# A mixed mLSTM, attention and expert layer: bias by VectorE, opening loads and router rearranged, and the first expert's products between the gathers

## The chip, the cores and the metric

The kernel runs on one core of one Trainium2 chip. The metric is the device time of one execution in microseconds (us); lower is better. Engines are named TensorE (PE in the profile), VectorE (DVE), ScalarE (ACT), GpSimd (POOL) and SyncE (SP, which here only issues transfers).

## The reference

One decoder layer over 256 tokens of 2048 channels, all in fp32:

```python
h = rms_norm(x, norm1_g); z = h @ w_in              # 2048 x 11272
qk = silu(causal_dwconv([qm, km], conv_w))          # 4 taps
hm = sigmoid(om) * head_layernorm(mlstm(q, k, v, i, f))     # 4 heads of 256
ha = softmax(q @ k.T * dh**-0.5 + bias[rel_bucket]) @ v     # 8 heads of 128, causal
y = sigmoid(gm) * (hm @ w_branch_m) + sigmoid(ga) * (ha @ w_branch_a)
x = x + y @ w_out
t = rms_norm(x, norm2_g)
# group top-1 of 4, expert top-2 of 8 in it; 32 SwiGLU experts 2048 -> 256 -> 2048
x = x + sum_e w_e * (silu(t @ w1[e]) * (t @ w3[e])) @ w2[e]
out = rms_norm(x, final_g)
```

## The kernel before

All instructions are written out by hand for each engine; semaphores order them, and nothing is scheduled by a planner. An engine runs its instructions in the order of its own function.

**Projections.** The weights of `w_in`, the two branch matrices and `w_out` come in units of 256 columns, and each unit in two halves of 1024 rows (1 MB). SP loads a half into one of four raw buffers `wraw` (L395), ScalarE rounds it to fp32r in one of two buffers `wsplit` (L581), VectorE stores the remainder beside it (L1149, `split_half`), and TensorE multiplies the activations' two parts with the weights' two parts: two instructions for each of 8 row chunks, of 512 and 256 columns (`channel_half` L824, L826; `token_half` L840, L842). The two column halves of a bank are added by VectorE afterwards (L1158, `sum_halves`). TensorE takes some 5.5 us for a half.

**Opening.** ScalarE's queue issues nine small loads (L559 to L567: norm and convolution parameters, the gates' weight columns `wif_raw`, a broadcast bias `ifb`, the relative bias table, the bucket matrix and `g2T`). SP loads x in two halves and waits for all nine before the first weights (L389). ScalarE squares x (L572), GpSimd takes the root (L519), TensorE turns x with a diagonal matrix (L813), and `act_split` holds the normed, turned x. TensorE also spreads the bias table over distances with the bucket matrix (L803); VectorE copies the row (L1178), and SP stores it to DRAM and reads it back as `bias_flipped`, one shifted copy for each partition (L409, L412).

**Attention loop** (L908 on, four turns, each with two attention heads, one mLSTM head and eight halves of the gates' weights, `gate_half`). For each attention head TensorE adds the bias to the logits by products with a flip matrix (L920, L922); VectorE takes the maximum (L1324, L1325) and ScalarE the exponential (L662, L664).

**Output projection and router.** Eight units of `w_out`. For each, VectorE adds x (L1449, `x2u`), ScalarE copies it to `x2` and squares it (L725, L729), TensorE turns it (L984), ScalarE copies that (L713), and TensorE multiplies with the router's weights (L993) into a place for each unit. Then VectorE adds the units (L1496), scales with the root of the mean square (L1502), and chooses group and experts in some thirty short steps (`first_of` L1486 to L1490). ScalarE makes `h2n` and `h2hi` (L744, L746), GpSimd and VectorE the remainder `h2lo` (L552, L1528). TensorE ranks the tokens (L1026 to L1030), and VectorE makes the selection matrix `sel` (L1539 to L1542).

**Gather and experts.** 16 gathers (L1043), each four products of 512 columns into one of eight banks, bring the tokens into the order of their experts; ScalarE and VectorE copy the banks to `xg` in turn (L757, L1567). Where no expert has over 64 tokens, the short branch runs (`by_most` L360): 16 pairs of experts, in each `hidden` (L1056, w1 and w3, with two half-array products for each of 16 chunks), the gate, `rows` (L1084, w2) and `scatter` (L1100, L1101) of the pair before. SP loads w1 and w3 of an expert in an upper and a lower half of the rows (2 MB each), as TensorE gets done with the halves before, and w2 into two slots.

## Time and profile before

| | |
|---|---|
| median of 3 runs | 1272.96 us (1272.76 to 1274.13) |
| the profiled execution | 1268.82 us |
| its span | 1267.3 us |
| mean granted TensorE clock | 0.986 |
| busy: PE / PEld / DVE / ACT / POOL | 1183.3 / 886.9 / 689.1 / 413.2 / 44.9 us |
| moved by DMA | 336.52 MB, mean 266 GB/s |

The profile is one execution of the program. A row of the timeline gives start and length of an instruction and, in brackets, how long its engine had been idle and what ended that. Waiting of an engine costs time only where the others wait for it in turn. All times in the rows are from the span's start; the projections last to about 750 us, the router to 775, the gather to 791, and the experts to the end.

### The profile page before, as it was taken

Reading aid. Unit: us, or ns where it says so; the run is one execution under the profiler, and the core shown is the slowest. Engines: PE = TensorE matmul, PEld = TensorE weight load, DVE = VectorE, ACT = ScalarE, POOL = GpSimd, SP = SyncE. Lnnn points to the kernel's source line nnn. Section 1 sums busy time; section 2 is a strip of 40 time slices with the busy share of each in tenths; the row PEclk is TensorE's granted clock in tenths of the full one; section 3 lists DMA queues with packets and bytes.
Section 4 is the critical chain, followed back from the end, with each engine's and each line's share of the span. In section 5 each row is a group of like instructions: output and inputs, shape, how many; then the busy total and the mean of one; then the engine's idle time right before and its main releaser. Section 6 shows DMA issues by size and latency. Waiting matters only on the chain.

```text
span 1267.3 us, 19180 instructions
## 1 busy us (share of the span) xinstructions
PE 1183.3 (93%) x7194; PEld 886.9 (70%) x7194; DVE 689.1 (54%) x980; ACT 413.2 (33%) x463; POOL 44.9 (4%) x57
## 2 busy tenths in 40 slices
PE   5999999999999999999999985899999999899995
PEld 4888888888888888888888875555554544444442
DVE  4678555554666657567875547243444433433335
ACT  4444333334334354443344443111111211111113
POOL 1000000001002022000000002000000000000000
PEclk9999999999999999999999987999999999999998
DMA  7765565655555455555765635899999999999993
GB/s 245 226 190 175 166 193 172 195 174 178 185 165 167 134 164 165 165 166 182 251 177 181 236 148 226 342 402 425 426 426 425 425 425 425 425 425 424 425 425 150
DMA packets 170146, 336.52 MB, mean 266 GB/s; under 512 B 12144, under 2 KB 136192, under 8 KB 153088
## 3 DMA queue, kind: packets, MB, share of 16 engines
q1 hardware_dynamic: 163088, 335.58, 71.8%
q10 hardware_dynamic: 7024, 0.48, 0.4%
q8 instruction: 22, 0.36, 0.1%
q14 instruction: 12, 0.10, 0.0%
HBM read 333.93 MB, written 2.11 MB: 265 GB/s over the span
## 4 chain that ended last, share of the span: by engine, by line
PE 56%; issue 39%; ACT 1%; DVE 1%; ACTq 1%; POOL 1%; POOLq 0%; DVEq 0%
PE ps L824 19%; PE ps L840 11%; PE ps L826 10%; PE ps L842 6%; PE ps L973 5%; PE ps L974 2%; PE ps L813 1%; POOL h2lo L552 1%; PE ps L942 0%; PE ps L993 0%; ACTq L564 0%; DVE wsplit L1149 0%; ACT xsq L572 0%; ACT h2n L744 0%; ACT wsplit L581 0%
## 5 line engine op out<-in xcount | busy, mean ns | idle before, releaser
L1149 DVE TENSOR_TENSOR wsplit<-wraw,wsplit 128x2048 fp32r<-128x2048 f32 x120 | 277.1, 2309 | 180.5 <-ACT wsplit L581 179.7
L824 PE MATMUL ps<-act_split,wsplit 128*128 128x512 f32 x1024 | 360.7, 397 | 0.0
L581 ACT ACTIVATE wsplit<-wraw 128x2048 fp32r<-128x2048 f32 x120 | 230.0, 1917 | 386.7 <-PE ps L826 204.7
L826 PE MATMUL ps<-act_split,wsplit 128*128 128x256 f32 x1024 | 286.6, 280 | 0.0
L840 PE MATMUL ps<-wsplit,act_split 128*128 128x512 f32 x640 | 226.8, 398 | 2.1 <-DVE wsplit L1149 2.1
L824 PEld LDWEIGHTS ps<-act_split,wsplit 128*128 128x128 f32 x1024 | 192.0, 188 | 46.1 <-DVE wsplit L1149 1.3
L826 PEld LDWEIGHTS ps<-act_split,wsplit 128*128 128x128 f32 x1024 | 193.3, 189 | 0.2
L842 PE MATMUL ps<-wsplit,act_split 128*128 128x256 f32 x640 | 179.2, 280 | 0.0
L840 PEld LDWEIGHTS ps<-wsplit,act_split 128*128 128x128 f32 x640 | 120.1, 188 | 31.3 <-issue 2.7
L1056 PE MATMUL ps<-w_a,xe 128*64 128x256 f32 x1024 | 115.4, 381 | 13.8 <-DMA w_a<-in_w_dram 12.0
L1595 DVE TENSOR_TENSOR hid<-sg,ps 128x128 f32<-128x128 f32 x32 | 9.2, 288 | 206.0 <-ACT sg L769 206.0
L842 PEld LDWEIGHTS ps<-wsplit,act_split 128*128 128x128 f32 x640 | 120.8, 189 | 0.0
L1056 PE MATMUL ps<-w_b,xe 128*64 128x256 f32 x1024 | 115.8, 381 | 0.0
L1056 PEld LDWEIGHTS ps<-w_a,xe 128*64 128x64 f32 x1024 | 72.5, 137 | 61.6 <-DMA w_a<-in_w_dram 21.2
L1084 PE MATMUL ps<-w_a,hidT 128*64 128x512 f32 x256 | 113.3, 595 | 0.4 <-ACT hidT L772 0.4
L1084 PE MATMUL ps<-w_b,hidT 128*64 128x512 f32 x256 | 113.3, 595 | 0.0
L1056 PEld LDWEIGHTS ps<-w_b,xe 128*64 128x64 f32 x1024 | 71.3, 137 | 41.6 <-issue 4.3
L1620 DVE TENSOR_TENSOR x<-x,ps 128x512 f32<-128x512 f32 x128 | 85.0, 684 | 9.0 <-PE ps L1101 6.8
L973 PE MATMUL ps<-br_split,wsplit 128*128 128x512 f32 x256 | 88.8, 394 | 0.0
L1084 PEld LDWEIGHTS ps<-w_a,hidT 128*64 128x64 f32 x256 | 33.7, 137 | 70.0 <-issue 68.9
L1100 PE MATMUL ps<-ys_hi,slot_of 128*128 128x512 f32 x128 | 61.0, 477 | 18.8 <-DVE x L1620 18.8
L769 ACT ACTIVATE sg<-ps 128x128 f32<-128x128 f32 x32 | 8.9, 277 | 198.4 <-PE ps L1056 198.4
(274 smaller groups left out, 1082.0 us busy)
## 6 DMA issues: line engine op xcount, KB each, us to landing
w_a<-in_w_dram SPq DMA_DIRECT2D x96, 1024.0 KB, 19.0
w_b<-in_w_dram SPq DMA_DIRECT2D x96, 1024.0 KB, 21.3
wraw<-in_w_in_dram SPq DMA_DIRECT2D x88, 1024.0 KB, 5.1
wraw<-in_w_out_dram SPq DMA_DIRECT2D x16, 1024.0 KB, 5.1
wraw<-in_w_branch_m_dram SPq DMA_DIRECT2D x8, 1024.0 KB, 5.1
wraw<-in_w_branch_a_dram SPq DMA_DIRECT2D x8, 1024.0 KB, 5.1
xin<-in_x_dram SPq DMA_DIRECT2D x2, 1024.0 KB, 6.5
x<-in_x_dram SPq DMA_DIRECT2D x1, 2048.0 KB, 9.3
```

What stands on the lines that cost most here:

```text
L581: act.activation(wsplit[:, q % 2, :, 0], wraw[:, q % RAW], ACT.Copy).then_inc(rounded, 1)
L824: pe.matmul(banks[b], w[:, k, 0, b * P:(b + 1) * P], a, start=first and k == 0, stop=False)
L826: last = pe.matmul(banks[b][:, 0:T], w[:, k, 1, b * P:(b + 1) * P], a[:, 0], start=False, stop=last_half and k == HALF_K - 1)
L840: pe.matmul(banks[t], a[:, 0, t * P:(t + 1) * P], w[:, k], start=first and k == 0, stop=False)
L842: last = pe.matmul(banks[t][:, 0:UNIT], a[:, 1, t * P:(t + 1) * P], w[:, k, 0], start=False, stop=last_half and k == HALF_K - 1)
L973: pe.matmul(bank, w[:, k, 0, b * P:(b + 1) * P], a, start=k == 0, stop=False)
L974: last = pe.matmul(bank[:, 0:T], w[:, k, 1, b * P:(b + 1) * P], a[:, 0], start=False, stop=k == HALF_K - 1)
L1056: last = pe.matmul(ps[f * SLOTS:(f + 1) * SLOTS, 0, 0:2 * P].rearrange("p (w f) -> p w f", w=2), xe[:, b, k], w13[b][:, :, k, f * P:(f + 1 ...
L1084: last = pe.matmul(ps[b * SLOTS:(b + 1) * SLOTS, 2 + n], hidT[:, b, f * SLOTS:(f + 1) * SLOTS], w2s[slot][b][:, f, n * 512:(n + 1) * 512], ...
L1100: pe.matmul(ps[:, 6 + g % 2], to_tokens, ys_hi[:, n * 512:(n + 1) * 512], start=True, stop=False)
L1149: dve.tensor_tensor(wsplit[:, q % 2, :, 1], wraw[:, q % RAW], wsplit[:, q % 2, :, 0].bitcast(F32), ALU.subtract).then_inc(split, 1)
L1620: dve.tensor_tensor(cols, cols, ps[:, 6 + g % 2], ALU.add).then_inc(added, 1)
```

## The change

1. *Opening.* ScalarE issues four loads, the other five follow the first four weight loads on SP (`late_loaded`). VectorE squares the second half of x. The product with the bucket matrix stands behind the first four halves, the copies for it and for the gates behind the first pair of convolution units. Twelve products of the identity with itself (`WARM`) stand ahead of all. The bias row goes to DRAM and back behind the twelve following weight loads.
2. *Attention.* The flip matrix goes. VectorE adds `bias_at` to the logits, reading and writing backwards along the row; ScalarE's exponential reads the sum from SBUF.
3. *Output projection and router.* ScalarE and VectorE split the unnormed x2 into `x2hi` and `x2lo`, unit by unit. The router's products add up over the units in two banks. The last unit's halves of a bank are no longer summed: it takes three products of 256 columns in place, and VectorE adds x to the bank and squares the sum. GpSimd's subtraction (`h2lo`) goes. The starts of the experts come from a scan over the counts.
4. *Gather.* As x2 isn't normed, a product with the roots (`rms_rep`) gives a factor for each slot, `slot_rms`; the tokens are multiplied with it when taken from `xg`. There are 17 gathers over six banks. The first expert's chunk products run three gathers behind.
5. *Loads.* w1 and w3 lie by halves, so the second expert's upper half can be loaded once two raw buffers are free. w2 of experts 1, 2 and 3 is loaded ahead of the gather, that of expert 0 behind it.

The core of the diff:

```diff
 @block.sync
-            sp.wait_ge(par_loaded, 16 * 9)
             pair(COL_QK, None)
+            sp.dma_start(wif_raw[:], ...).then_inc(late_loaded, 16)
...
+            pairs(1, UNITS_QK, COL_QK, 0)
             sp.wait_ge(rev_ready, 1)
             sp.dma_start(rev_dram, rev[:]).then_inc(rev_stored, 16)
             sp.wait_ge(rev_stored, 16)
-            pairs(1, UNITS_QK, COL_QK, 0)
...
             for kh in range(2):
                 load_hidden(0, 0, kh)
-            sp.wait_ge(used, HALVES)
-            for kh in range(2):
-                load_hidden(1, 1, kh)
-            load_rows(0, lambda b: b)
+            for kh in range(2):
+                sp.wait_ge(split, HALVES + 2 * kh - 2)
+                load_hidden(1, 1, kh)
+            sp.wait_ge(used, HALVES - 1)
+            load_rows(0, lambda b: b, (1,))
+            sp.wait_ge(used, HALVES)
+            load_rows(1, lambda b: b + 2, (1,))
             sp.wait_ge(routed, 1)
+            sp.wait_ge(x2lo_ready, UNITS_OUT)
             load_rows(1, lambda b: b + 2, (0,))
-            sp.wait_ge(xg_summed, DC)
-            load_rows(1, lambda b: b + 2, (1,))
 @block.tensor
+            for n in range(WARM):
+                pe.matmul(ps[:, 6, 0:P], ident[:], ident[:], start=True, stop=True)
-                    pe.matmul(bank[:, 0:P], q_h[:, 0:P], k_h[:, 0:P], start=True, stop=False)
-                    pe.matmul(bank[:, 0:P], flip[:], bias[:, 0, P:T], start=False, stop=True)
-                    pe.matmul(bank[:, P:REV], q_h[:, P:T], k_h[:], start=True, stop=False)
-                    pe.matmul(bank[:, P:REV], flip[:], bias[:, 0], start=False, stop=True).then_inc(logits, 1)
+                    pe.matmul(bank[:, 0:P], q_h[:, 0:P], k_h[:, 0:P], start=True, stop=True)
+                    pe.matmul(bank[:, P:REV], q_h[:, P:T], k_h[:], start=True, stop=True).then_inc(logits, 1)
+            def gather_with_first_hidden():
+                done = 0
+                for n in range(COMMON_GATHERS, DC + 1):
+                    gather(n)
+                    if gathers[n] is not None and gathers[n] >= BEHIND:
+                        first_hidden(done)
+                        done += 1
+                for k in range(done, DC):
+                    first_hidden(k)
 @block.gpsimd
-                pool.tensor_tensor(h2lo[:, t, cols], h2n[:, t, cols], h2hi[:, t, cols].bitcast(F32),
-                                   ALU.subtract).then_inc(h2lo_ready, 1)
 @block.vector
+                    dve.tensor_tensor(prob[:, a, P - 1::-1], ps[:, 4 + a, P - 1::-1], bias[:, 0:P], ALU.add)
+                    steps.done(dve.tensor_tensor(prob[:, a, REV - 1:P - 1:-1], ps[:, 4 + a, REV - 1:P - 1:-1], bias[:, 0:T],
+                                                 ALU.add))
...
-            dve.tensor_tensor(mk[:, :, 0], oh[:, :, 0], oh[:, :, 1], ALU.add)
-            steps.done(dve.tensor_tensor(rt[:, 1], iota_t, by_token(FIRST, EXPERTS), ALU.is_gt))
-            dve.tensor_tensor(mk[:, :, 1], rt[:, 3], rt[:, 1], ALU.add).then_inc(mk_ready, 1)
+            dve.tensor_tensor(mk[:], oh[:, :, 0], oh[:, :, 1], ALU.add).then_inc(mk_ready, 1)
...
-                    dve.tensor_copy(xe[:, b], xg[:, :, ds(at, SLOTS)]).then_inc(xe_ready, 1)
+                    factors = slot_rms[:, ds(at, SLOTS)].unsqueeze(1).to_broadcast([P, DC, SLOTS])
+                    dve.tensor_tensor(xe[:, b], xg[:, :, ds(at, SLOTS)], factors,
+                                      ALU.mult).then_inc(xe_ready, 3 - len(experts))
```

How the order of instructions changes at three places. First SP's queue at the start, before (L388 is x, L395 the weight halves):

```order
L388 DMA xin<-in_x_dram 128x2048 x2
L395 DMA wraw<-in_w_in_dram 128x8x256 [waits par_loaded]
L395 DMA wraw<-in_w_in_dram 128x8x256 x3
L409 DMA rev_dram<-rev 8x384 [waits rev_ready]
L412 DMA bias_flipped<-rev_dram 128x256 [waits rev_stored]
L412 DMA bias_flipped<-rev_dram 128x256 x7
```

and now:

```order
L401 DMA xin<-in_x_dram 128x2048 x2
L407 DMA wraw<-in_w_in_dram 128x8x256 x4
L419 DMA wif_raw<-in_w_in_dram 128x16x8
L420 DMA ifb<-in_if_bias_dram 128x8
L421 DMA relb<-in_rel_bias_dram 32x8
L422 DMA onehot_s<-in_onehot_dram 32x256
L423 DMA g2T<-in_norm_g_dram 128x16
```

The first weights wait for nothing, and store and reloading of the bias row are gone from here. On TensorE at the start, before:

```order
L802 MATMUL ps<-ident,param_rows 128x104 [waits par_loaded,consts_ready]
L803 MATMUL ps<-onehot_s,relb 8x256
L813 MATMUL ps<-diag,xin 128x128 [waits normed,x_loaded_1,x_loaded_0,rev_ready,param_ready]
L813 MATMUL ps<-diag,xin 128x128 x31
L824 MATMUL ps<-act_split,wsplit 128x512 [waits split,bank_free]
```

and now:

```order
L834 MATMUL ps<-ident 128x128 [waits ident_ready]
L834 MATMUL ps<-ident 128x128 x11
L836 MATMUL ps<-ident,param_rows 128x104 [waits par_loaded]
L845 MATMUL ps<-diag,xin 128x128 [waits x_loaded_1,normed,x_loaded_0,param_ready]
L845 MATMUL ps<-diag,xin 128x128 x31
L856 MATMUL ps<-act_split,wsplit 128x512 [waits split,bank_free]
```

The turning of x no longer stands behind the bias row (`rev_ready`). On TensorE at the end of the gather, before (`w_a` holds w1 and w3 of the first expert):

```order
L1043 MATMUL ps<-sel,h2lo 128x512
L363 TENSOR_LOAD most_i [waits table_ready]
L363 ISA x2
L364 COMPARE_AND_BRANCH
L1056 MATMUL ps<-w_a,xe 64x256 [waits w13a_upper_loaded,hid_ready,xe_ready]
L1056 MATMUL ps<-w_a,xe 64x256 x15
```

and now, one of the thirteen stretches (`xe_first` holds the first expert's tokens, chunk by chunk):

```order
L1098 MATMUL ps<-sel,x2hi 128x512 [waits gathered_even]
L1098 MATMUL ps<-sel,x2lo 128x512
L1098 MATMUL ps<-sel,x2hi 128x512
L1098 MATMUL ps<-sel,x2lo 128x512
L1113 MATMUL ps<-w_a,xe_first 64x256 [waits first_xe_ready]
L1113 MATMUL ps<-w_a,xe_first 64x256
```

The branch with its load of `most_i` now stands behind the third gather, and the first expert's 32 products come in pairs between the gathers.

## Rows read from the trace of the kernel before

**Rows 1.** By stage: stretch, length, busy PE PEld DVE ACT POOL, PEclk, DMA share, GB/s.

```profile
400.00:560.00 160.00, 160.00 (x923) 139.90 (x922) 101.62 (x163) 70.37 (x76) 16.37 (x15) 1.00 0.50 157
900.00:1200.00 300.00, 278.28 (x1893) 148.52 (x1891) 120.93 (x226) 51.38 (x85) 0.00 (x0) 1.00 1.02 425
```

**Rows 2.** Timeline of the opening: start, length, engine, line, operation, [idle before].

```profile
3.50 4.80 ACTq L564 DMA_DIRECT2D ifb<-in_if_bias_dram  x1
11.06 1.91 ACT L572 ACTIVATE xsq<-xin 128x2048 f32<-128x2048 f32 x1
14.98 0.17 DVE L1163 TENSOR_SCALAR stat<-stat 128x2 f32<-128x2 f32 x1 [8.70 <-ACT xsq L572]
17.06 8.85 PE L813 MATMUL ps<-diag,xin 128*128 128x128 f32 x64 [4.57 <-DVE rev L1178]
```

**Rows 3.** Timeline of TensorE in one turn of the attention loop.

```profile
407.29 0.39 PE L920 MATMUL ps<-bias_flipped,flip 128*128 x2
407.51 0.60 PE L921 MATMUL ps<-qk_now 128*128 128x256 f32 x2
407.95 0.59 PE L922 MATMUL ps<-bias_flipped,flip 128*128 x2
```

**Rows 4.** Timeline of VectorE from the last output unit to the mask.

```profile
750.83 1.29 DVE L1158 TENSOR_REDUCE osum<-ps 128x256 f32<-128x512 f32 x2 [6.32 <-PE ps L842]
752.16 0.69 DVE L1449 TENSOR_TENSOR x2u<-x,osum 128x512 f32<-128x512 f32 x1
756.85 0.82 DVE L1496 TENSOR_REDUCE rt<-ps 128x72 f32<-128x288 f32 x2 [1.86 <-issue]
762.08 4.10 DVE L1521 TENSOR_TENSOR sc<-sc 128x2 f32<-128x2 f32 x1
766.10 2.57 DVE L1486 SCALAR_TENSOR_TENSOR rt<-rt,sc,iota_e 128x32 f32<-128x32 f32 x2
769.61 0.22 DVE L1525 TENSOR_TENSOR mk<-rt 128x64 fp32r<-128x64 f32 x1
```

**Rows 5.** Timeline of GpSimd at the router.

```profile
761.66 6.80 POOL L552 TENSOR_TENSOR h2lo<-h2n,h2hi 128x2048 fp32r<-128x2048 f32 x2 [5.90 <-ACT h2hi L746]
```

**Rows 6.** The instructions that read x's tile, and its load's time to landing.

```profile
L813 PE MATMUL ps<-diag,xin x64: 274/275/552, 17.1 to 25.6; 128*128 128x128 f32 x64
DMA to landing us min/median/max: 5.0/6.5/7.9
```

**Rows 7.** Costliest groups of the page: VectorE's split of a weight half.

```profile
L1149 DVE TENSOR_TENSOR wsplit<-wraw,wsplit 128x2048 fp32r<-128x2048 f32 x120 | 277.1, 2309 | 180.5 <-ACT wsplit L581 179.7
```

**Rows 8.** Timeline of VectorE in the same turn of the loop.

```profile
412.91 0.41 DVE L1325 TENSOR_REDUCE stat<-ps 128x1 f32<-128x256 f32 x1
417.79 1.29 DVE L1158 TENSOR_REDUCE gates<-ps 128x512 f32 x2 [3.94 <-PE ps L826]
```

**Rows 9.** Waits of SP's queue, 0 to 60 us. Columns: total, times, longest.

```profile
SPq L412 <- DMA rev_dram<-rev: 5.5, 1, 5.5
```

**Rows 10.** Timeline of TensorE from the gather to the second expert.

```profile
774.96 0.80 PE L1043 MATMUL ps<-sel,h2hi 128*128 128x512 f32 x1 [3.79 <-DVE sel L1542]
778.25 0.40 PE L1043 MATMUL ps<-sel,h2hi 128*128 128x512 f32 x1
791.30 0.39 PE L1043 MATMUL ps<-sel,h2lo 128*128 128x512 f32 x1
793.43 7.13 PE L1056 MATMUL ps<-w_a,xe 128*64 128x256 f32 x64 [1.74 <-DVE xe L1581]
801.99 7.13 PE L1056 MATMUL ps<-w_b,xe 128*64 128x256 f32 x64
```

**Rows 11.** Timeline of TensorE, first whole-array product behind an expert's half-array products.

```profile
824.75 0.50 PE L1100 MATMUL ps<-ys_hi,slot_of 128*128 128x512 f32 x1
```

**Rows 12.** Costliest groups of the page: weight loads of one expert.

```profile
L1056 PEld LDWEIGHTS ps<-w_a,xe 128*64 128x64 f32 x1024 | 72.5, 137 | 61.6 <-DMA w_a<-in_w_dram 21.2
```

**Rows 13.** One stretch: length, busy PE (x), PEclk, DMA share, GB/s.

```profile
820.00:822.00 2.00, 2.00 (x22) 1.00 0.05 20
```

More of the change, by code:

```diff
@@ L51 @@
 PAIR_HALVES = 4
+WARM = 12
 UNITS_QK = 2 * M_WIDTH // UNIT
@@ L497, in _ @@
                 pool.sem_inc(primed, 1)
-            for m in (ident, flip, before, mask_ts, mask_st, pick):
+            steps.done(pool.memset(ident[:], 0.0))
+            pool.affine_select(out=ident[:], in_=ident[:], compare_op=ALU.not_equal, fill=1.0, base=0,
+                               pattern=[[-1, P]], channel_multiplier=1).then_inc(ident_ready, 1)
+            for m in (before, mask_ts, mask_st, pick):
                 last = pool.memset(m[:], 0.0)
@@ L1015, in _ @@
             pe.wait_ge(wrt_ready, 1)
-            with pe.Fori(1, UNITS_OUT // 2) as i:
+            out_pair(1)
+            with pe.Fori(2, UNITS_OUT // 2 - 1) as i:
                 out_pair(i)
+            out_pair(UNITS_OUT // 2 - 1, end=True)
+            route(UNITS_OUT // 2 - 1, 0)
             turn_x2(1, UNITS_OUT - 1)
-            for u in range(2):
-                last = route(UNITS_OUT // 2 - 1, u)
-            last.then_inc(routed, 1)
+            route(UNITS_OUT // 2 - 1, 1).then_inc(routed, 1)
@@ L1037, in _ @@
-            parts = [part[:].rearrange("p t (q c) -> p t c q", c=DC) for part in (h2hi, h2lo)]
-            for c in range(DC):
-                if c >= 8:
-                    pe.wait_ge((xg_act, xg_dve)[c % 2], (c - 8) // 2 + 1)
-                for t in range(TT):
-                    for n, part in enumerate(parts):
-                        last = pe.matmul(ps[:, c % 8], part[:, t, c], sel[:, t], start=t == 0 and n == 0,
-                                         stop=t == TT - 1 and n == 1)
-                last.then_inc(xg_summed, 1)
+            pe.wait_ge(x2lo_ready, UNITS_OUT)
@@ L1105, in experts @@
                 if chunks > 1:
+                    for n in range(COMMON_GATHERS, DC + 1):
+                        gather(n)
                     with pe.Fori(0, EXPERTS // 4) as j:
@@ L1116, in experts @@
                     return
-                for b in range(2):
-                    hidden(0, 0, b)
-                    turn(0, b)
+                gather_with_first_hidden()
+                turn(0, 0)
+                hidden(0, 0, 1)
+                turn(0, 1)
                 rows(0, 0, 0)
@@ L1302, in _ @@
             dve.wait_ge(o_ready, 1)
-            with steps.loop(0, M_HEADS, 9) as i:
+            dve.wait_ge(flip_loaded, 16 * A_HEADS)
+            with steps.loop(0, M_HEADS, 11) as i:
                 def ahead(q):
```

314 lines of the change are left out of this document (205 added, 109 removed).

## The prediction

> **What bounds the kernel now.** I read the busy time by stage first. While the projections run, TensorE has no gap: 160.00 us of 160 at 400 to 560 us, VectorE at 101.62 and the DMA engines at half their time. From 900 to 1200 us the DMA engines stand at 1.02 of their time and move 425 GB/s, with TensorE at 278 of 300 [rows 1]. So the kernel has two bounds, TensorE up to the router and the stream of expert weights behind it, and between them, at 750 to 820 us, neither: a chain over VectorE, ScalarE, GpSimd and short products. What the change takes from TensorE before the router counts in full. What it takes from the chain counts as far as it lets the weight stream start earlier, since from there the bytes set the end.
>
> Three places matter. **The opening:** ScalarE's queue is held 4.80 us by the issue of the bias load at 3.50, so its first square starts only at 11.06. The mean squares are complete at 14.98, and TensorE turns x from 17.06 [rows 2]. **The attention loop:** each of 8 heads has two products with the flip matrix [rows 3]. **The router:** VectorE's step at 762.08 takes 4.10 us for 128x2 elements and the next pair 2.57 at 766.10, while GpSimd subtracts from 761.66 to 768.46 [rows 4, 5].
>
> **The change, part by part** (gains are minus).
>
> *Opening, -4.5.* x's second half was issued at 1.3 and its load took at most 7.9 [rows 6], so it landed by 9.2. ScalarE now issues four loads, and squares the first half alone. VectorE squares the second in about 2.3 us (its 128x2048 split, [rows 7]): 11.5. From the mean square to the first transpose was 2.08 us, in which the copies of the parameters and of the bias row stood too; those are gone from there, so 1.5. TensorE starts at 13.0, or 12.3 if x lands 0.7 earlier without the small packets beside it. Between the two I take 12.6, so -4.5. Bounds: -3.5 (full 2.08, no earlier landing) and -6.2, where x lands early and the transposes begin at full rate. They now begin at half: one lasts up to 552 ns against 275 in the middle [rows 6]. The 12 warming products run from about 3 us and then TensorE idles for some 5 us, as it did before; I take nothing for them. The first weight load moves from 11 us to 1.7 us and is ready before TensorE asks. Behind the four weight loads stand the late loads. Their first reader on TensorE comes after four halves, at some 43 us, so they cost nothing; if they were late, TensorE would wait there.
>
> *The bucket product, +0.4,* now stands in TensorE's full stretch: 256 columns take 0.44 us as L921 to L922 show [rows 3].
>
> *Bias on VectorE, -5.2.* The product of 128 columns holds TensorE 0.22 us (407.29 to 407.51), the one of 256 columns 0.43 to 0.44. That is 0.65 for a head, 8 heads, 5.2 us. VectorE gains four additions per loop turn; as the maximum over the same 256 columns takes 0.41 [rows 8] and over 128 columns about 0.3, they take 1.4 us. Behind them VectorE sat idle 3.94 us until TensorE was done [rows 8], so they are covered; without that cover they would cost 1.4 a turn. Bounds: -3.9 (a third of a microsecond lost each turn) and -5.3. What was loaded through DRAM at the start moves behind twelve weight loads. SP waited 5.5 us for that store [rows 9]; with the issue of store and bias loads I put it at 8 us on the next weight load. Its slot falls free some three halves of 5.5 us before TensorE needs it, so it is hidden, with about 8 us to spare.
>
> *Small edits before the router, +0.3:* two casts of 128x128 now stand ahead of a split that TensorE waits for. The extra splits of x2 (0.69 each, [rows 4]) and the second copies on ScalarE fall into idle time of 2 to 4 us per half; if it were gone, each would cost its own length.
>
> *Router to choice, -8.5.* The last unit is summed in place: 1.29 and 0.69 [rows 4] become about 0.85, of which the product for the unit before, still in TensorE's order, leaves 0.9. The 0.82 for unit sums at 756.85 and one of two pairs of scalings go, 1.25. Together -2.2. Without GpSimd's subtraction, the pair of rows at 762.08 and 766.10 shrinks from 6.6 us to 0.6, and two comparisons ahead of the mask go: from 762.08 to the mask's end (769.83) 7.75 becomes 1.35, with 0.15 before it, so -6.5. The scan of starts adds 0.2.
>
> *Gather, +5.0.* Before, it was 27.0 us from the first gather product at 774.96 to the second expert's first at 801.99 [rows 10]. Now: 64 products at 0.237 (778.25 to 791.30, 55 steps), 15.1; 1.5 lost in a slow start (eight steps took 3.3); two fp32 row products of 512 columns, 1.7, and the short one 0.4; the first expert's products, 7.1 as at 793.43; the branch, which now stands between gathers, 0.5 (between 0 and the 1.7 it could hide in before); and 13 switches between whole-array and half-array products. One such switch at 824.75 lengthens the first product from 0.40 to 0.50 [rows 11]; with the way in I take 0.25 each, 3.2. That is 29.5. Then the gap before the second expert: 1.4 before, and about 1.1 more, because VectorE now makes the second expert's tokens (128x1024 with a factor, some 1.2) and the mixing after the gather, ahead of the gate. So 32.0 against 27.0.
>
> The switches' bounds are 0 and what full exposure of the weight loads costs: 16 pairs of products, 4 loads of 137 ns each [rows 12], 8.8 us. In a long run the trace shows them hidden: 64 loads of 137 ns in 7.13 us [rows 10]. The Trainium skill (TensorE: Matmul & The Clock Gate, The mechanism) says that a weight load overlaps a running product only when its row group differs, and here all have all rows. The long run doesn't agree with it, but a lone pair is not a long run.
>
> *From there to the end, 0.* The stream waits once more for TensorE: at 820 to 822 the DMA share is 0.05 [rows 13]. As both kernels have loaded the same by then, that restart, and with it the end, moves with the second expert's start. Router plus gather: -8.5 + 5.0 = -3.5 (bounds -8.2 and +2.1).
>
> **Sum:** -4.5 + 0.4 - 5.2 + 0.3 - 3.5 = **-12.5 us**. Against the profiled execution's own 1268.82 that is 1256.3. That execution lies 4.1 below the median of the runs shown, 1272.96, and I put the forecast against the median: **1260.5**.
>
> **Rivals.** (1) *The interleaving eats its gain:* each pair's weight loads are exposed, 8.8 for my 3.2, +5.6: 1266.1. For it, the skill's rule; against it, the long run. 0.15. (2) *All goes through:* switches and branch cost next to nothing, the gap stays at 1.4, and the transposes start at full rate: -3.2, -0.5, -1.1, -1.7 more, 1254.0. For it, products in the trace that switch width without a visible idle time. 0.15. (3) *The 6 us at the router are not GpSimd's:* something else holds VectorE there, and the steps stay long. Then 6.0 less is gained, 1266.5. Against it, the two rows begin and end with GpSimd's two. 0.05. (4) *Slower than before:* the additions write and read backwards. If a step backwards is much dearer than forwards, VectorE comes late in each of four loop turns, and TensorE stands. VectorE has 3.9 us idle and 1.4 us of additions planned; beyond 5.3 us for the four, each further microsecond costs four. It turns the result when they take about 5.3 + 12.5 / 4 = 8.4 us, six times my estimate, and at 9.5 us gives 1277. No row has a backward step, so only implausibility speaks against it: 0.03. That the interleaving doesn't happen at all is excluded by the order of instructions above.
>
> **How the numbers follow.** The forecast has 0.62. The range takes in rivals 1 and 3 nearly whole and most of rival 2: 1254.5 to 1266.5. A measurement of this kernel tells 0.2% (2.5 us) from no change. My own case and rivals 1 to 3 all gain over 6 us; several small misses at once could leave under 2.5, 0.02. So faster 0.95, same 0.02, slower 0.03.
>
> **What would show it.** TensorE's first transpose at 12 to 13.5 us instead of 17.06. The loop of four turns 1.3 us shorter per turn, with VectorE's idle time before the first gate sums near 2.5. No VectorE step over 1 us between the router and the mask, and the first gather product 8.5 us nearer to the last product of the output projection. The second expert's first product 32 us after the first gather product; 37 speaks for rival 1, 28 for rival 2. One gap in the stream of some 3 us, then 425 GB/s. I am wrong if TensorE shows idle time before a reader of the late loads, or at the loads behind the bias, or if the stream restarts no earlier against the router than before.

## The result and the profile after

| | before | changed |
|---|---|---|
| median of 5 runs, us | 1272.96 (1268.77 to 1274.13) | 1262.77 (1260.68 to 1264.67) |
| ratio to before | | 0.9924, 95% [0.9905, 0.9942] |
| the profiled execution, us | 1268.82, span 1267.3 | 1262.77, span 1261.0 |
| mean granted clock | 0.986 | 0.986 |

By the ratio the change is faster by 9.7 us (7.4 to 12.1). The forecast was 12.5 us of gain and 1260.5; the measured median lies 2.3 us above it and inside the range. The two traces differ by only 6.3 us, because the profiled execution of before was as fast as the fastest of its five. Stage by stage they say more than the total does:

| stage, by TensorE's and VectorE's rows | before | after | difference | predicted |
|---|---|---|---|---|
| start to first weight product | 25.67 | 22.66 | -3.0 | -4.5 |
| to the first logits of the attention loop | 328.02 | 330.98 | +3.0 | +0.4 |
| to the last unit's sums | 397.14 | 392.21 | -4.9 | -4.9 |
| to the selection (first product on it) | 24.13 | 14.66 | -9.5 | -8.5 |
| to the second expert's first product | 27.03 | 34.24 | +7.2 | +5.0 |
| to the end | 465.3 | 466.2 | +0.9 | 0 |

Stages of the changed kernel (stretch, length, busy PE PEld DVE ACT POOL, PEclk, DMA share, GB/s); they answer to [rows 1]:

```profile
8.00:13.00 5.00, 0.41 (x2) 0.14 (x1) 2.88 (x6) 1.80 (x1) 0.71 (x1) 0.80 1.09 386
13.00:18.00 5.00, 4.62 (x22) 4.65 (x23) 3.41 (x5) 1.78 (x5) 0.00 (x0) 0.51 1.09 386
...
400.00:560.00 160.00, 160.00 (x921) 139.70 (x920) 108.08 (x177) 73.23 (x77) 16.39 (x15) 1.00 0.52 164
755.00:760.00 5.00, 1.25 (x5) 1.14 (x5) 4.46 (x17) 0.00 (x0) 0.00 (x0) 0.50 0.53 136
...
765.00:770.00 5.00, 5.00 (x23) 3.61 (x22) 2.31 (x6) 1.38 (x2) 0.00 (x0) 0.96 0.01 3
...
900.00:1200.00 300.00, 277.79 (x1874) 147.56 (x1874) 129.73 (x226) 48.98 (x83) 0.00 (x0) 1.00 1.02 425
```

The two bounds are as before: TensorE without a gap up to the router, the weight stream at 425 GB/s behind it. New is the granted clock of 0.51 at 13 to 18 us; 0.50 is the lower of TensorE's two levels (1.2 GHz), 1.00 the upper (2.4 GHz).

The timeline of TensorE in the changed kernel, for [rows 2, 10]:

```profile
2.92 5.18 PE L834 MATMUL ps<-ident 128*128 128x128 f32 x24 [2.92 <-POOL ident L539]
8.91 0.31 PE L836 MATMUL ps<-ident,param_rows 104*128 104x104 f32 x1 [0.81 <-DMA param_rows<-in_norm_g_dram]
13.38 9.52 PE L845 MATMUL ps<-diag,xin 128*128 128x128 f32 x64 [4.17 <-DVE diag L1268]
22.66 0.48 PE L856 MATMUL ps<-act_split,wsplit 128*128 128x512 f32 x1
...
766.80 0.40 PE L1098 MATMUL ps<-sel,x2lo 128*128 128x512 f32 x1
767.13 0.65 PE L1113 MATMUL ps<-w_a,xe_first 128*64 128x256 f32 x4
767.71 0.61 PE L1098 MATMUL ps<-sel,x2hi 128*128 128x512 f32 x1
768.16 0.40 PE L1098 MATMUL ps<-sel,x2lo 128*128 128x512 f32 x1
...
790.69 1.95 PE L1113 MATMUL ps<-w_a,xe_first 128*64 128x256 f32 x16
794.52 0.30 PE L1160 MATMUL ps<-ident,hid 128*128 128x128 f32 x1 [1.89 <-DVE hid L1722]
```

Read the starts. Inside a kind the gather's products follow each other by 0.24 us. Into the first expert's four it is 0.33 (766.80 to 767.13), from there to the next gather product 0.58 against 0.45 for four in a long run (7.13 us for 64), and from that to its successor 0.45. So a step, four gather products and the first expert's four, takes 1.83 us and not 1.39: 0.44 for each pair of switches, out of the gather and back into it.

The last eight products of the router, in the changed kernel and then in the kernel before:

```profile
749.13 1.08 PE L1037 MATMUL ps<-wrt,x2T 128*128 128x36 f32 x8 [0.75 <-ACT x2T L742]
```

```profile
754.84 1.92 PE L993 MATMUL ps<-wrt,x2T 128*128 128x36 f32 x8 [0.24 <-ACT x2T L713]
```

The same eight last 1.08 us in six of the fourteen traces of this study and 1.55 to 1.93 in eight, and one program does both: the kernel before has 1.92, experiment 1 with the same router 1.08. So 0.8 us of the stage from the sums to the selection is chance.

VectorE's timeline in the changed kernel, for [rows 4, 8]:

```profile
9.44 2.28 DVE L1263 SCALAR_TENSOR_TENSOR xsq<-xin 128x2048 f32<-128x2048 f32 x1
...
12.76 0.48 DVE L1268 TENSOR_SCALAR diag<-ident,stat 128x128 f32<-128x128 f32 x2 [0.83 <-POOL stat L560]
...
411.02 0.41 DVE L1421 TENSOR_TENSOR prob<-ps,bias_at 128x256 f32<-128x256 f32 x1
...
415.10 1.29 DVE L1248 TENSOR_REDUCE gates<-ps 128x512 f32 x2 [1.84 <-PE ps L858]
...
745.85 0.76 DVE L1586 TENSOR_TENSOR x2u<-ps,x 128x256 f32<-128x256 f32 x2 [3.99 <-PE ps L874]
...
754.08 0.16 DVE L1632 TENSOR_TENSOR sc<-sc 128x2 f32<-128x2 f32 x1
754.16 0.41 DVE L1606 SCALAR_TENSOR_TENSOR rt<-rt,sc,iota_e 128x32 f32<-128x32 f32 x2
...
755.12 0.22 DVE L1634 TENSOR_TENSOR mk<-oh 128x64 fp32r<-128x64 f32 x1
```

The steps of 4.10 and 2.57 us are 0.16 and 0.41. A backward addition over 256 columns takes 0.41 us, what a maximum over them takes, and VectorE still idles 1.84 us before the first gate sums of a turn, where it idled 3.94. A turn of the attention loop is 51.9 us instead of 53.2.

### The profile page after: what moved, and what is told of

It reads as the page before. It is cut to its first block, busy times and chain, and to the rows that moved or that the text cites. A ratio compares the mean times of both kernels' runs of the same rounds, so it can differ in the third digit from the quotient of the medians.

```text
span 1261.0 us, 19243 instructions
## 1 busy us (share of the span) xinstructions
PE 1194.1 (95%) x7226; PEld 889.5 (71%) x7226; DVE 710.0 (56%) x1022; ACT 408.1 (32%) x462; POOL 37.9 (3%) x53
## 4 chain that ended last, share of the span: by engine, by line
PE 57%; issue 40%; DVE 1%; DMA 0%; ACT 0%; ACTq 0%; POOL 0%; POOLq 0%; DVEq 0%
PE ps L856 19%; PE ps L885 10%; PE ps L858 10%; PE ps L887 5%; PE ps L1017 5%; PE ps L1018 2%; PE ps L845 1%; DMA param_rows<-in_norm_g_dram 0%; PE ps L986 0%; PE ps L1037 0%; DVE wsplit L1239 0%; PE ps L872 0%; ACT wsplit L608 0%; PE ps L874 0%; PE ps L873 0%
## 5 line engine op out<-in xcount | busy, mean ns | idle before, releaser
L885 PE MATMUL ps<-wsplit,act_split 128*128 128x512 f32 x608 | 216.2, 400 | 2.3 <-DVE wsplit L1239 2.3
L887 PE MATMUL ps<-wsplit,act_split 128*128 128x256 f32 x608 | 170.4, 280 | 0.0
L885 PEld LDWEIGHTS ps<-wsplit,act_split 128*128 128x128 f32 x608 | 114.2, 188 | 31.0 <-issue 2.7
L1142 PE MATMUL ps<-w_a,xe 128*64 128x256 f32 x960 | 108.5, 381 | 12.4 <-DMA w_a<-in_w_dram 12.4
L887 PEld LDWEIGHTS ps<-wsplit,act_split 128*128 128x128 f32 x608 | 114.8, 189 | 0.0
L1142 PEld LDWEIGHTS ps<-w_a,xe 128*64 128x64 f32 x960 | 67.9, 137 | 58.3 <-DMA w_a<-in_w_dram 22.3
## 6 DMA issues: line engine op xcount, KB each, us to landing
w_a<-in_w_dram SPq DMA_DIRECT2D x96, 1024.0 KB, 18.3
```

The lines of the kernel that those rows point to most:

```text
L885: pe.matmul(banks[t], a[:, 0, t * P:(t + 1) * P], w[:, k], start=first and k == 0, stop=False)
L887: last = pe.matmul(banks[t][:, 0:UNIT], a[:, 1, t * P:(t + 1) * P], w[:, k, 0], start=False, stop=last_half and k == HALF_K - 1)
L1142: last = pe.matmul(ps[f * SLOTS:(f + 1) * SLOTS, 0, 0:2 * P].rearrange("p (w f) -> p w f", w=2), xe[:, b, k], w13[b][:, k // HALF_K, :, k ...
```

## The experiments

Each was timed in five rounds, four to six runs, beside the kernel before, and ratios are to it. The first number of each result is its median in us; in square brackets stands the 95% interval of the ratio. A "pair" below is a wide (512 columns) and a narrow (256) product on a weight half, in a row; its time is taken from start to start. It has two levels, 0.347 and 0.353 us, at the same granted clock.

**1. The bias alone.** The kernel before with these edits and their counterparts in table, offset and exponentials:

```diff
-                    pe.matmul(bank[:, 0:P], flip[:], bias[:, 0, P:T], start=False, stop=True)
-                    pe.matmul(bank[:, P:REV], flip[:], bias[:, 0], start=False, stop=True).then_inc(logits, 1)
...
+                    dve.tensor_tensor(prob[:, a, P - 1::-1], ps[:, 4 + a, P - 1::-1], bias[:, 0:P], ALU.add)
```

> The kernel before, with the bias added on VectorE as the change does it and nothing else of the change. Theory A (the prediction's term): the four bias products of a turn leave TensorE and each turn of the attention loop is 1.3 us shorter, four turns 5.2 us: 5.2 us under the kernel before, ratio 0.996. Rival B: part of the shorter turn in the trace of the change was the wide and narrow products running closer together there (0.3466 us a pair in place of 0.3534), not the bias; then the bias alone gives 4 us or less. Rival C (the fourth rival of the prediction): the backward additions fill VectorE's idle time and a turn gets longer; then 0 to 4 us slower. The trace also tells whether the weight stage before 110 us stays at 0.3466 us a pair and falls to 0.3534 after the small products of L871, as in the one trace of the kernel before: if these levels are set by the program, they come at the same places again; if they are chance, they come elsewhere.

1266.50, ratio 0.9953 [0.9940, 0.9966]: 6.0 us faster (4.3 to 7.6), the profiled execution's loop 51.85 us a turn. The prediction's term of 5.2 stands, and rival 4 falls. The levels of the pairs stood where the kernel before has them up to 300 us (0.3467 to 110, 0.3533 behind it). From 302 us on they did not: 0.3534 here, 0.3466 there, in a program that is the same up to there.

**2. The bucket product moved.** In the changed kernel, behind the stage of q and k instead of in front of its loop; its two waits, VectorE's copy and SP's reload moved with it:

```diff
-            pe.matmul(ps[0:A_HEADS, 6, 0:T], relb[:], onehot_s[:], start=True, stop=True).then_inc(rev_summed, 1)
             stage(channel_half, 0, 1, UNITS_QK)
+            pe.matmul(ps[0:A_HEADS, 6, 0:T], relb[:], onehot_s[:], start=True, stop=True).then_inc(rev_summed, 1)
```

> The changed kernel, with the bucket product moved from behind the first four halves of weight products (45 us) to just before the products of the gate columns (113 us), its copy and the reload of the bias moved behind it. Theory A: in the trace of the change each pair of wide and narrow products takes 0.3534 us from the bucket product on, 0.3466 before it, and in the kernel before the slow level begins only at the gate columns; the small product sets the level. Then the pairs between 45 and 113 us take 0.3466 again, 1.3 us less, and, if the level after 302 us is also as in the kernel before, 1.0 us less there: 1.3 to 2.3 us under the change, ratio to before about 0.991 where the change has 0.992. Rival B: the level is chance or belongs to the other edits of the opening; then the stage stays at 0.3534 or changes without the move, and the total is that of the change within 0.7 us.

The wide product of a pair at 60 to 110 us (min/median/max ns), first in the changed kernel:

```profile
L856 PE MATMUL ps<-act_split,wsplit x143: 395/398/403, 59.8 to 110.0; 128*128 128x512 f32 x143
```

With the bucket product moved:

```profile
L856 PE MATMUL ps<-act_split,wsplit x145: 391/391/391, 59.8 to 109.7; 128*128 128x512 f32 x145
```

And one stretch of the same kernel (columns as in [rows 1]; the third number from the end is the granted clock):

```profile
300.00:310.00 10.00, 10.00 (x47) 8.35 (x46) 3.21 (x3) 5.75 (x4) 4.04 (x2) 0.83 0.62 205
```

The stage from the first weight product to the gate columns, which holds the bucket product in both, took 89.46 us, 90.84 in the changed kernel: the 1.4 us of theory A are there. But the median, 1263.25 (0.9923 [0.9909, 0.9936]), shows none of it. In this trace a stretch at half the granted clock, behind 301 us, took 1.5 us; it also stands in the traces of three other kernels of this study at that place (5, 6 and best), and not in the rest. Why it comes is open. Of the seven traces with the product at its old place three are at the slow level before they come to it, and in those the move can give nothing. The second part of A, a gain behind 302 us, failed: the level there was 0.3534.

**3. The first expert's steps apart**, and **4. in groups of four.** In the changed kernel, G = 16 and G = 4:

```diff
...
                 for n in range(COMMON_GATHERS, DC + 1):
                     gather(n)
-                    if gathers[n] is not None and gathers[n] >= BEHIND:
-                        first_hidden(done)
-                        done += 1
+                    due += gathers[n] is not None and gathers[n] >= BEHIND
+                    if due - done >= G:
+                        for k in range(done, due):
+                            first_hidden(k)
+                        done = due
```

> The changed kernel with the first expert's 16 steps on w1 and w3 all behind the gather instead of one behind each of its products; everything else as changed. Theory A: what the interleaving costs is the change between the two kinds of product, 0.44 us for each of 13 steps (1.83 us a step against 0.944 + 0.446 alone), 5.7 us; it hides nothing but the wait for the first expert's tokens, since TensorE is busy throughout: without it 3.5 to 5.5 us faster than the change (some of it lost to a wait of about 1 us before the first or the last step). Rival B: the steps are long for another reason (waits for the copies out of the banks, 0.44 us each, which stay without the interleaving): then within 1 us of the change or slower by the 1 to 2 us that the interleaving hides.

> The changed kernel with the first expert's steps on w1 and w3 put behind every fourth gather product, four at a time. Theory A (a price for each change of kind): 3 or 4 changes of kind in place of 13, 0.44 us each: 4 us faster than the change, nearly all of what having them apart gives, with the last steps still hidden beside the last copies. Rival B (the price is each step's own): the same time as the change within 0.7 us.

TensorE with the steps apart:

```profile
762.08 1.12 PE L1084 MATMUL ps<-sel,rms_rep 128*128 128x64 f32 x4 [3.86 <-DVE sel L1656]
...
781.84 7.13 PE L1113 MATMUL ps<-w_a,xe_first 128*64 128x256 f32 x64
790.15 0.30 PE L1162 MATMUL ps<-ident,hid 128*128 128x128 f32 x1 [1.19 <-DVE hid L1724]
```

In groups of four:

```profile
768.65 0.40 PE L1098 MATMUL ps<-sel,x2lo 128*128 128x512 f32 x1
768.98 1.95 PE L1113 MATMUL ps<-w_a,xe_first 128*64 128x256 f32 x16
770.85 0.61 PE L1098 MATMUL ps<-sel,x2hi 128*128 128x512 f32 x1
771.30 0.40 PE L1098 MATMUL ps<-sel,x2lo 128*128 128x512 f32 x1
```

Apart: 1257.66, 0.9875 [0.9859, 0.9892]; fours: 1257.62, 0.9886 [0.9869, 0.9902]. From the selection to the second expert 28.3 us and 30.2 us, where the change has 34.2. Four steps at a time pay at their edges 0.09, 0.09 and 0.21 us over the plain spacing, one step pays 0.09, 0.13 and 0.21. So the price belongs to the switch. The changed kernel has twelve blocks with a way in and a way back, and a thirteenth with the way in alone, behind the last gather: 12 times 0.44 and 0.09 are 5.4 us. Apart only one way in is left, which makes 5.3 us of the 5.9 between the two traces. The other 0.7 is the gap before the second expert, 1.19 us with the steps apart and 1.89 in the change: VectorE's tokens and mixing and ScalarE's table load now run beside the first expert's products. The interleaving as made costs more than it hides: without it the kernel is 5 us faster by the medians and 6 by the ratios, whose intervals don't meet. No wait that it could have hidden appears: the first expert's products follow the last gather product within 0.33 us.

**5. Without the warming products** (WARM = 0):

> The changed kernel without the twelve products of the identity at the start. Theory A (the prediction's): they are worth nothing and cost nothing; the transposes start at 13.4 us as in the change and the total is the same within 0.5 us. Rival B: the twelve products, and the idle time behind them, are what brings the granted clock to 0.50 from 11 to 18 us in the trace of the change, where the kernel before, with an idle engine up to 11 us, shows 1.00 throughout and has its slow transposes for about 3 us of 8.85; then without them the transposes take 8.9 us in place of 9.0 to 10.3 and the first weight product starts 0.2 to 1.4 us earlier than in the changed kernels so far (22.1 to 23.4 us).

TensorE's timeline without them:

```profile
13.52 8.71 PE L845 MATMUL ps<-diag,xin 128*128 128x128 f32 x64 [4.17 <-DVE diag L1268]
21.98 0.47 PE L856 MATMUL ps<-act_split,wsplit 128*128 128x512 f32 x1
```

1264.43, 0.9933 [0.9921, 0.9946]: no difference that the runs resolve. In its trace the transposes take 8.71 us and the record of the granted clock stays at 1.00, as rival B said. The six traces with the twelve products have 0.50 on record from 10 to 13 us on, until 16 to 20, and 8.9 to 10.3 us of transposes. By the traces the twelve cost 0.2 to 1.6 us and give nothing.

**6. GpSimd's subtraction put back** in the changed kernel, at the router, its result unused:

```diff
+            pool.wait_ge(used, HALVES)
+            pool.wait_ge(x2hi_ready, UNITS_OUT)
+            pool.tensor_tensor(copy_of[:], x2[:, 0], x2[:, 1], ALU.subtract).then_inc(copied, 1)
...
+            pe.wait_ge(copied, 1)
```

> The changed kernel with one subtraction of 128x2048 numbers on GpSimd put back beside VectorE's router steps (its result is not used). In the kernel before a GpSimd subtraction of that size ran for 6.8 us from 761.66 us, and two VectorE steps beside it took 4.10 and 2.57 us where the same steps take 0.2 to 0.4 us in the changed kernel. Theory A (the prediction's 6.5 us): GpSimd's subtraction is what holds the VectorE steps; the change gives back what it took away, one or two router steps last 2 to 6 us again and the total is 4 to 6.5 us over the changed kernel. Rival B (the third rival of the prediction): the steps were long for another reason (data that ScalarE had not yet written, the two comparisons); then the router steps stay under 0.7 us each and the total is that of the change within 0.7 us, or longer only by what a wait for the subtraction's end adds.

VectorE and then GpSimd of this kernel:

```profile
751.60 0.42 DVE L1620 SCALAR_TENSOR_TENSOR lr<-ps,stat,brt 128x36 f32<-128x36 f32 x2 [2.96 <-PE ps L1041]
752.06 0.16 DVE L1624 TENSOR_REDUCE sc<-lr 128x2 f32<-128x8 f32 x1
752.25 3.34 DVE L1625 TENSOR_SCALAR sc<-sc 128x2 f32<-128x2 f32 x1
...
751.07 4.50 POOL L593 TENSOR_TENSOR copy_of<-x 128x2048 f32<-128x2048 f32 x1 [1.66 <-ACT x2hi L762]
```

A step of 0.17 us lasts 3.34 and ends when GpSimd ends (755.57). TensorE's wait for `copied` stands before the gather, at 765, and holds nothing. The selection comes 18.3 us after the last sums, 14.7 in the change: 3.2 of that are this step, and 0.5 the last eight router products, 1.55 us long here and 1.08 there, which is chance (see the profile after). Total 1264.96, 0.9941 [0.9929, 0.9954]: 2 us over the change, in other rounds and with intervals that overlap, and not the 4 to 6.5 that I expected. So the trace carries the finding, not the total. Rival 3 falls.

My 4 to 6.5 us rested on a misreading of [rows 5]. The 6.80 us there are two subtractions:

```profile
L552 POOL TENSOR_TENSOR h2lo<-h2n,h2hi 128x2048 fp32r<-128x2048 f32 x1 | 4.5, 4502 | 5.9 <-ACT h2hi L746 5.9
L552 POOL TENSOR_TENSOR h2lo<-h2n,h2hi 128x1024 fp32r<-128x1024 f32 x1 | 2.3, 2337 | 0.0
```

This run put the first one back, and it takes 4.50 us in both kernels. In the kernel before VectorE's step of 4.10 us ends at 766.18, with the first subtraction (766.16), and the pair of 2.57 ends at 768.67, one short step after the second (768.46).

Two kinds of VectorE step beside a subtraction were not held, one that reads the banks and a maximum. The Trainium skill (GPSIMD Engine Reference, 1. Specifications) says that GpSimd's memory interfaces are shared with VectorE, with contention for VectorE instructions in a two-port mode or with two inputs from SBUF. The trace of the kernel before agrees for the steps with two SBUF inputs (L1521, 4.10 us; L1486, 2.57). The step held here has one, and no trace shows whether it ran in that mode.

**7. Idle time filled**, on the kernel with the steps apart, and WARM = 14:

```diff
+            def busy(products):
+                for n in range(products):
+                    pe.matmul(ps[:, 6, 0:P], ident[:], ident[:], start=True, stop=True)
...
+            busy(12)
             pe.wait_ge(param_ready, 1)
...
+            busy(16)
             pe.wait_ge(mk_ready, 1)
...
             last.then_inc(rank_summed, 1)
+            busy(14)
```

> The kernel with the first expert's steps apart (1257.7 us), with products of the identity that nobody reads while TensorE would wait: 14 at the start and 12 behind the transpose of the parameters, 16 while VectorE chooses the experts, 14 while it makes the selection. In all traces so far the granted clock falls to 0.50 once the engine has idled for some us, about 752 us, and comes back 5 us into the gather, whose products take 0.63 us each until then and 0.40 afterwards. Theory A: with the idle time filled the clock stays at 1.00 over the router, the gather's first 5 us are at full speed, 2 to 2.5 us less there, and the 64 transposes of the opening take under 8 us in place of 9.0 to 10.3, 1.5 to 3 us less: 1253 us. Rival B: the fillers run into the real products (each is up to 0.43 us long at the low clock) and delay them, or VectorE gets slower beside them; then 0 to 1.5 us slower than the kernel without them.

TensorE's timeline with the idle time filled:

```profile
13.34 7.38 PE L851 MATMUL ps<-diag,xin 128*128 128x128 f32 x64 [1.47 <-DVE diag L1278]
20.48 0.48 PE L862 MATMUL ps<-act_split,wsplit 128*128 128x512 f32 x1
...
758.45 0.66 PE L1092 MATMUL ps<-sel,rms_rep 128*128 128x64 f32 x4 [0.74 <-DVE sel L1664]
758.92 0.59 PE L1106 MATMUL ps<-sel,x2hi 128*128 128x512 f32 x1
...
784.41 0.30 PE L1170 MATMUL ps<-ident,hid 128*128 128x128 f32 x1 [1.20 <-DVE hid L1732]
```

1252.55, 0.9842 [0.9828, 0.9855], 5 us under the kernel with the steps apart (4 by the ratios, whose intervals don't meet). From 8 to 800 us the mean granted clock is 1.00. The transposes take 7.38 us and the second expert comes 26.2 us after the selection, 28.3 without. The selection comes 14.2 us after the last sums, 15.5 without; but the kernel best below, with the same fillers, has 15.5 too, 0.8 of it from the last router products (1.92 us there, 1.08 here). Here the fillers end 1.5 us before the transposes; the change's twelve end at 8.1 us and leave 4.2 us idle in front of them.

**8. The mixing moved** from behind the second expert's tokens into the gather (VectorE):

> The changed kernel with VectorE's four products of mix (0.98 us) moved from behind the second expert's tokens to the middle of the gather. In the trace of the change they stand between the tokens (792.88) and the silu (793.77) that TensorE waits for (1.89 us idle). Theory A: the wait shortens by 0.9 us and the total by 0.9. Rival B: the steps in the middle of the gather delay a copy out of a bank that TensorE needs; VectorE waits 0.9 to 1.6 us there between steps, so I expect no such loss, at most 0.3 us.

ScalarE and VectorE at the end of the gather, with the mixing moved:

```profile
791.38 0.69 ACT L789 ACTIVATE xg<-ps,g2T 128x512 f32<-128x512 f32 x1 [2.98 <-PE ps L1098]
...
792.38 1.28 ACT L796 ACT_TABLE_LOAD   x1 [0.31 <-issue]
...
793.79 0.26 ACT L801 ACTIVATE sg<-ps 128x128 f32<-128x128 f32 x1
794.08 0.29 DVE L1728 TENSOR_TENSOR hid<-sg,ps 128x128 f32<-128x128 f32 x1 [0.53 <-ACT sg L801]
```

1261.66, 0.9914 [0.9900, 0.9928]: not to be told from the change (0.9924). TensorE's gap went from 1.89 to 1.61 us, not by 0.9. VectorE now waits for ScalarE, which loads its table for the sigmoid for 1.28 us behind the last copy of the gather. That load had run beside the mixing all along; in the kernel with the steps apart it runs beside products.

**9 to 12. The best version and the level of the pairs.** Kernel 7 with the move of kernel 2; then the same with one product of the identity behind each of three small products; that kernel again; and with the second of the three alone:

```diff
             last.then_inc(if_products, 1)
+            busy(1, 7)
...
             last.then_inc(if_summed, 1)
+            busy(1, 7)
...
             pe.matmul(ps[:, 5, 4:8], upto[:], lst[:, 1], start=False, stop=True).then_inc(cum_summed, 1)
+            busy(1, 7)
```

> The kernel with the idle time of TensorE filled (1252.6 us) and, beside that, the bucket product moved behind the first weight stage as in bucket_late. Theory A: where the stage starts at 0.3466 us a pair, the bucket product no longer brings it to 0.3534, 1.4 us less in such an execution; but three of the four traces of the changed kernel without that early start (0.3534 from the first product on) say that the start is chance, so over the runs 0 to 1.4 us less: 1251.2 to 1252.6 us. Rival B: the move costs (the reload of the bias waits behind later loads): 0.5 us or more slower.

> The kernel best, with one product of the identity (0.23 us) behind each of three small products of the weight stages (gate columns, their folding, the cumulated sums). The level of the pairs has changed, in all traces, only where other products stand between them. Theory A (which of two levels follows is set by how many products stand between, as if by parity): one more brings the level back, and the pairs behind 118 us take 0.3466 in place of 0.3534: up to 2 per cent of 190 us, 3.7 us less. Rival B (it is not a count that sets it): the level stays at 0.3534 and the kernel is 0.7 us slower by the three products, within the noise of best.

> The kernel nudge once more, for a second trace of it. Its one trace shows 0.3533 us a pair from 112 to 140 us, 0.3467 from there to 292 us, where best shows 0.3533 up to 297 us, and the median was 1.9 us under best's. Theory A (the program sets the level): the levels stand at the same places again and the median is 1.5 to 3 us under best's 1251.4. Rival B (chance): they come elsewhere, and the median is within 1 us of best's.

> The kernel best with only the one product behind the folding of the gate columns. Theory A (a count or place that the program sets): the pairs take 0.3467 us from about 140 us on, as in the trace of nudge, since nothing ahead of that place differs but the one product that left the level at 0.3533 there; then about as fast as nudge. Rival B (chance): no such step at that place, within 1 us of best.

The wide product at 150 to 200 us in the kernel best:

```profile
L862 PE MATMUL ps<-act_split,wsplit x143: 395/398/403, 149.7 to 199.9; 128*128 128x512 f32 x143
```

With the three products:

```profile
L862 PE MATMUL ps<-act_split,wsplit x146: 392/394/395, 149.6 to 199.9; 128*128 128x512 f32 x146
```

With the one behind the folding:

```profile
L862 PE MATMUL ps<-act_split,wsplit x145: 392/395/395, 149.8 to 199.7; 128*128 128x512 f32 x145
```

| kernel | median | ratio to before |
|---|---|---|
| best | 1251.39 | 0.9834 [0.9821, 0.9848] |
| three products | 1249.51 | 0.9819 [0.9802, 0.9836] |
| the same again | 1250.41 | 0.9834 [0.9813, 0.9855] |
| one product | 1250.17 | 0.9828 [0.9807, 0.9849] |

In all three traces with the extra product the pairs take 0.3467 us from 140 to 292 us, where best, the change and the kernel before have 0.3533. From the gate columns to the small product with `pick` at 294 us that is 184.4 to 184.6 us against 187.0. So the program does set the level there, and one product behind the folding is enough. Behind that place the three traces are at 0.3533 and best at 0.3467, which gives back some 1 us. The medians lie 1.0 to 1.9 us under best's and the ratios 0 to 1.9, which the intervals don't separate from none. Best itself is 21 us under the kernel before and 11 under the change.

## Why the prediction was right, and where it was off

**The loop and the bias: right.** -4.9 by the traces for -4.9, -6.0 (4.3 to 7.6) for the bias by itself. The additions took 1.38 us of 3.94 us of idle time, as reckoned. The sign "near 2.5" for what is left was too high, 1.84: I took the additions off the 3.94, but not the 1.3 us by which the turn itself gets shorter.

**Router to choice: right in mechanism; the 1 us over the forecast is mostly luck.** From the last sums to the first logits 4.5 us in place of 6.9, from there to the mask 5.0 (750.32 to 755.34) in place of 12.1. That is -2.4 and -7.1, -9.5 together, for my -2.2, -6.5 and +0.2 for the scan. But 0.8 of the 2.4 is the last eight router products, 1.92 us in the one trace and 1.08 in the other, by chance; the second pair of scalings, 0.4, which I had in the 2.2, falls in the 7.1. Without that luck it is -8.7 for -8.5. The 6 us of the two long steps were GpSimd's: they end with its two subtractions, and experiment 6 brings such a step back.

**Gather: +7.2 for +5.0, a term mis-sized.** "With the way in I take 0.25 each, 3.2": it is 0.44 for each of twelve pairs of switches and 0.09 for a last way in, 5.4. I read only the first product behind a switch, 0.10 longer [rows 11]; the price has three parts, before the half-array products, before the first whole-array product and before the second. Rival 1, at 8.8, had all weight loads exposed. The Trainium skill's rule behind it (TensorE: Matmul & The Clock Gate, The mechanism) would expose them in every run of products; the runs show 0.44 us where the kind changes and none within 64 products in 7.13 us. Beyond that the short row product and the slow start cost some 0.9 more than I gave them, both at half the clock; the branch without a visible cost (0.5) and a gap of 2.1 for 2.5 gave that back.

**Opening: -3.0 for -4.5, both steps off.** The transposes start at 13.38, not 12.6: later than the 13.0 that I had without x landing earlier, though inside the bound of -3.5 taken alone. "In which the copies of the parameters ... stood too; those are gone from there": one copy was not gone but had moved ahead of VectorE's square, and waits for the parameters, which land at 8.9 us. The square starts at 9.44 for it, while x had landed by 8.7 (issued by 1.3, 7.4 at most on the way). No run put the copy behind the square, so those 0.8 us are read from the rows and not tested. Then the transposes last 9.52 us and not 8.85, and -3.0 lies outside my bounds. "I take nothing for" the warming products was wrong by 0.8 us in this trace (8.71 us of transposes without them, experiment 5) and by up to 1.6 in others; experiment 7 shows what they can give when more of the wait is filled.

**To the loop: +3.0 for +0.4, not foreseen.** The bucket product cost some 0.7 us and not 0.4, since the pairs beside it stretch. And it left the pairs behind it at 0.3534 us and not 0.3467: 68 us at 2% are 1.3. At 302 us the traces differ by the same 2% over 52 us, 1.0. The first of the two is the change's (experiments 2 and 9 to 12, and four of four traces with the product at its place that came to it at the fast level). The second is chance: before and bias_alone differ in it.

**To the end: +0.9 for 0.** Stream and restart behave as forecast: from the second expert's first product to the next issue of w1 and w3 (821.57 and 814.34) it is 19.58 us before and 19.59 after. Where in the last 446 us the difference lies is not found; the stage takes 464.4 to 468.0 us in the fourteen traces, so one trace of each kernel can't resolve it.

The medians, 10.2 apart, lie nearer to the sum of 12.5 than the two traces, 6.3 apart. The trace of before had the fast level behind 302 us, and its execution was as fast as the best of its five; how often its others had it no trace says. So the sum by stages rests on one execution of each kernel, and chance of some 1 us stands in two of its terms, with opposite signs: +1.0 behind 302 us and -0.8 at the router.

## What to carry to other kernels

Price work that is threaded into other work by the number of changes of kind, and take that price from the starts of three products in a row, not from the length of one. Threading pays only where it hides a wait that the trace shows. Where TensorE waits some us before a dense stretch, either fill nearly the whole wait (1.5 us were left in experiment 7) or leave it empty: the fillers that ended 4.2 us early left it slower for longer than none, by the traces. And before a difference between two traces is put down to a change, compare the same stage in other traces of the same instructions: here that moved 0.8 us from mechanism to chance.

## What the runs showed of the hardware that I had not expected

**Two levels of a regular stream at one granted clock.** Pairs of a 512-column and a 256-column product run at 0.3466 or at 0.3534 us, clock 1.00 in both. VectorE's sums, one unit of 32 pairs apart, show it, first in the kernel before:

```profile
41.27 1.28 DVE L1158 TENSOR_REDUCE pre<-ps 128x256 f32<-128x512 f32 x2
...
52.36 1.28 DVE L1158 TENSOR_REDUCE pre<-ps 128x256 f32<-128x512 f32 x2
```

and behind the bucket product in the changed kernel:

```profile
72.64 1.28 DVE L1248 TENSOR_REDUCE pre<-ps 128x256 f32<-128x512 f32 x2
...
83.95 1.28 DVE L1248 TENSOR_REDUCE pre<-ps 128x256 f32<-128x512 f32 x2
```

11.09 us against 11.31. In these traces the level changes only where other products stand between pairs. At some places every trace changes alike (bucket product, folding with one more product), at others the same program comes out at either level: at the first pair, where three of fourteen traces start slow, and behind 302 us, where three of the eleven that come at the slow level leave at the fast one. What sets it is not settled: a plain count of products is one reading of the folding, but the chance cases speak against it as the whole cause.

**At the start the record of the granted clock is not the pace.** In the kernels that leave TensorE idle there the record reads 1.00 throughout, but their first 12 to 14 transposes start 0.21 us apart and the later ones 0.11. The twelve warming products do the same at a record of 1.00: 24 instructions in 5.18 us, 0.21 apart until 7.6 us. With the twelve and a wait behind them the record reads 0.50 for some 6 us, and 15 to 28 transposes are slow. With experiment 7's fillers all transposes but the first start 0.11 apart. So read the pace at the start from the spacing of equal products; there is no sign that an idle engine keeps the full clock.

**A small VectorE step can wait out a GpSimd instruction:** 0.17 us became 3.34, and 0.16 became 4.10. In each of the three cases the held step ends with GpSimd's instruction, so the loss is what is left of that instruction, however small the step. Not every step is held: a maximum, and one that reads the banks, ran beside it at their usual length.
